# Low parts of the modulation's weight chunks on VectorE, and each modulation row spread one row later, in a two-layer diffusion block

## The reference

```python
def hybrid_layer(x, ctx, c, c_ctx, lw, pos, update_ctx):
    mod_x = jax.nn.silu(c) @ lw['ada_w'] + lw['ada_b']
    mod_c = jax.nn.silu(c_ctx) @ lw['ada_w'] + lw['ada_b']
    shift, scale, gate = jnp.split(mod_x[:, None, :], 3, axis=-1)
    c_shift, c_scale, c_gate = jnp.split(mod_c, 3, axis=-1)
    h = rmsnorm(x, lw['norm_w']) * (1 + scale) + shift
    ...
    x = x + gate * merge_branches(o_m, o_s, o_a, z_m, z_s, z_a, g, lw)
    ...
    # merge_branches, last two lines
    y = jax.nn.sigmoid(g_m) * y_m + jax.nn.sigmoid(g_s) * y_s + jax.nn.sigmoid(g_a) * y_a
    return y @ lw['w_out']
```

## Time and profile before

| | us |
|---|---|
| median of 3 runs | 2136.12 |
| lowest and highest of them | 2133.67, 2136.14 |
| span of the profiled execution | 2133.4 |
| PE busy | 1837.2 (86%) |
| DVE busy | 1210.5 (57%) |
| ACT busy | 889.6 (42%) |
| POOL busy | 602.6 (28%) |

### The profile page before, as it was taken

One profiled execution on the slowest core, in us unless ns is written; L12 is line 12 of the kernel. 1 busy time (PEld: TensorE's weight loads), 2 busy tenths in 40 slices (PEclk: granted clock), 3 DMA queues, 4 the chain that ended last, 5 costly groups with the idle time before them and its releaser, 6 DMA issues.

```text
span 2133.4 us, 27538 instructions
## 1 busy us (share of the span) xinstructions
PE 1837.2 (86%) x10845; PEld 1573.3 (74%) x10845; DVE 1210.5 (57%) x2334; ACT 889.6 (42%) x1679; POOL 602.6 (28%) x328
## 2 busy tenths in 40 slices
PE   5398998879999899998888958989869997899888
PEld 2276787768898788897767946678757886788668
DVE  1524686786666576665232342467867677676334
ACT  1222454544545455544222131344545455555332
POOL 0322221212221222113445132221303323232552
PEclk9699999989999999999999979899989999999999
DMA  6210110101111111113334112011101221122442
GB/s 213 60 46 20 31 27 22 40 11 40 51 50 41 35 35 45 30 41 113 114 103 139 60 62 58 21 34 26 34 20 50 65 65 45 39 61 60 133 138 80
DMA packets 192287, 125.90 MB, mean 59 GB/s; under 512 B 21468, under 2 KB 187934, under 8 KB 192158
## 3 DMA queue, kind: packets, MB, share of 16 engines
q1 hardware_dynamic: 187248, 108.57, 18.0%
q10 hardware_dynamic: 3630, 11.37, 1.4%
q0 software_dynamic: 1280, 4.20, 0.6%
HBM read 119.92 MB, written 4.19 MB: 58 GB/s over the span
## 4 chain that ended last, share of the span: by engine, by line
PE 66%; DVE 19%; ACT 7%; POOL 4%; issue 3%; DMA 1%; ACTq 0%; DVEq 0%; SPq 0%
PE acc L1138 50%; PE wide L1161 5%; PE ptp L1177 4%; DVE nmax L1676 3%; PE pv L1190 3%; DVE e L1693 3%; PE pv L1191 3%; POOL w_lo L1489 2%; DVE pt L1698 2%; ACT e L1402 1%; DVE k_s L1279 1%; ACT w_hi L1321 1%; DVE swapped L1588 1%; DVE rot L1589 1%; DVE q_s L1279 1%
## 5 line engine op out<-in xcount | busy, mean ns | idle before, releaser
L1489 POOL TENSOR_TENSOR w_lo<-w_raw,w_hi 128x1024 fp32r<-128x1024 f32 (+6 forms) x220 | 462.9, 2113 | 1191.3 <-ACT w_hi L1321 1191.1
L1138 PE MATMUL acc<-h_hi,w_hi 128*128 128x512 f32 (+2 forms) x1288 | 472.3, 367 | 43.1 <-POOL w_lo L1489 21.5
L1138 PE MATMUL acc<-h_lo,w_hi 128*128 128x512 f32 (+2 forms) x1288 | 468.2, 364 | 0.0
L1138 PE MATMUL acc<-h_hi,w_lo 128*128 128x512 f32 (+2 forms) x1288 | 466.5, 362 | 0.0
L1138 PEld LDWEIGHTS acc<-h_hi,w_hi 128*128 128x128 f32 (+1 forms) x1288 | 249.2, 194 | 86.0 <-issue 35.9
L1411 ACT ACTIVATE pt<-ptp 128x512 fp32r<-128x512 f32 (+3 forms) x312 | 166.2, 563 | 295.8 <-PE ptp L1177 295.2
L1138 PEld LDWEIGHTS acc<-h_hi,w_lo 128*128 128x128 f32 (+1 forms) x1288 | 248.5, 193 | 38.7 <-issue 1.5
L1138 PEld LDWEIGHTS acc<-h_lo,w_hi 128*128 128x128 f32 (+1 forms) x1288 | 249.1, 193 | 37.6 <-issue 1.3
L1676 DVE TENSOR_REDUCE nmax<-wide 128x1 f32<-128x768 f32 (+3 forms) x240 | 190.5, 794 | 130.7 <-PE wide L1161 129.1
L1321 ACT ACTIVATE w_hi<-w_raw 128x1024 fp32r<-128x1024 f32 (+6 forms) x220 | 199.8, 921 | 78.8 <-DMA w_raw<-in_w_out 67.1
L1402 ACT ACTIVATE e<-wide,nbias,rq 128x768 f32<-128x768 f32 x160 | 145.1, 907 | 172.4 <-DVE nbias L1682 171.8
(11 more groups left out here) (191 smaller groups left out, 3316.1 us busy)
## 6 DMA issues: line engine op xcount, KB each, us to landing
w_raw<-in_w_in SPq DMA_DIRECT2D x102, 512.0 KB, 3.7
w_raw<-in_ada_w SPq DMA_DIRECT2D x48, 512.0 KB, 4.3
w_raw<-in_w_out SPq DMA_DIRECT2D x16, 512.0 KB, 3.8
xres<-in_x ACTq DMA_DIRECT2D x2, 2048.0 KB, 11.2
w_raw<-in_w_o_mla SPq DMA_DIRECT2D x16, 256.0 KB, 2.8
w_raw<-in_w_o_swa SPq DMA_DIRECT2D x16, 256.0 KB, 2.8
w_raw<-in_w_o_ax SPq DMA_DIRECT2D x16, 256.0 KB, 2.8
w_raw<-in_mla_w_uq SPq DMA_DIRECT2D x16, 144.0 KB, 2.4
```

Of the source, the lines that this page charges most:

```text
L1138: ins = nc.tensor.matmul(dst, lhs, rhs, start=first, stop=last)
L1489: nc.gpsimd.tensor_tensor(w_lo[s][:, 0:k], w_raw[s][:, 0:k], f(w_hi[s][:, 0:k]), ALU.subtract).then_inc(w_lo_ready, 1)
```

## The change

`ada()` now returns a row's sums and its spread apart. In the merge, `late()` puts a row's sums down at once, then the spread of the row before it, and keeps its own for the next; the last is put down after the loop. At the head of the program a row is still sums and then spread. Spreads wait for their own row's copy (`row["v"]`) and no longer for everything read so far. The low parts of the rows' chunks (`ada`, 32 in the merges) are made by VectorE at the place of the W event in its order, counted by a semaphore of their own, `ada_lo_ready`; GpSimd makes all others.

```diff
@@ -456,19 +456,26 @@
             whole.update(cc)
         steps = list(group("ada", cost=1900, chunk_ids=cc, act=False, mode="adaF" if plain else "ada", l=l, j=j, slot=slot,
                            needs=lambda: dict(cs_ready=1))["steps"])
-        shape = dict(act=False, l=l, j=j, slot=slot, needs=lambda: dict(acc_free=n["free"], loads=(n["ada"] + 1) // 2))
+        row = {}
+
+        def made_row():
+            row["v"] = n["free"]
+
+        steps += step_of(made_row)
+        shape = dict(act=False, l=l, j=j, slot=slot, needs=lambda: dict(acc_free=row["v"], loads=made // 2 + 1))
+        spread = []
         if j < 2 * D // 256:
-            steps += group("adaT", mode="adaT", **shape)["steps"]
+            spread += group("adaT", mode="adaT", **shape)["steps"]
         else:
             for s in range(len(token_groups(l))):
-                steps += group("adaG", mode="adaG", s=s, **shape)["steps"]
+                spread += group("adaG", mode="adaG", s=s, **shape)["steps"]
         def read():
             ada_made[made] = n["acc"]
             if j == 2 * D // 256 - 1:
                 emit("MOD", l=l, free=n["free"])
                 n["mod"] += 1
-        return steps + [(read, 0)]
+        return steps, spread + [(read, 0)]
     def load_rows(l):
         def run():
@@ -526,7 +533,8 @@
             n["xl"] += 1
             load_table("s")
             for j in COLUMNS:
-                run_all(ada(0, j))
+                row, spread = ada(0, j)
+                run_all(row + spread)
                 if j in (3, 5):
                     norm_rows(0, (j - 3) // 2, 0)
             for tt in range(2, TT):
@@ -679,7 +687,14 @@
         flush()
-        merge = []
+        merge, put_off = [], []
+
+        def late(parts):
+            row, spread = parts
+            got = row + put_off
+            put_off[:] = spread
+            return got
+
         for t in range(KD):
             if t == KD - 2:
                 usable[0] = ROOMY
@@ -690,9 +705,10 @@
             if t == 0:
                 usable[0] = SLOTS
             if t % 2 == 0:
-                merge += ada(l, GATES[t // 2])
+                merge += late(ada(l, GATES[t // 2]))
             if l + 1 < LAYERS:
-                merge += ada(l + 1, t)
+                merge += late(ada(l + 1, t))
+        merge += put_off
         if l + 1 < LAYERS:
             load_table("s")
         run_all(merge)
@@ -846,7 +862,7 @@
         vec_done, vec_ready, consts_ready = semaphore("vec_done"), semaphore("vec_ready"), semaphore("consts_ready")
         cs_th, cs_ready, mod_ready = semaphore("cs_th"), semaphore("cs_ready"), semaphore("mod_ready")
-        w_hi_ready, w_lo_ready = semaphore("w_hi_ready"), semaphore("w_lo_ready")
+        w_hi_ready, w_lo_ready, ada_lo_ready = (semaphore(k) for k in ("w_hi_ready", "w_lo_ready", "ada_lo_ready"))
         acc_done, ev_a, acc_free = semaphore("acc_done"), semaphore("ev_a"), semaphore("acc_free")
         h_done, l_done = semaphore("h_done"), semaphore("l_done")
@@ -936,10 +952,12 @@
         for c in range(len(chunks)):
             loads[c] = (0 if slot_prev[c] is None else loads[slot_prev[c]]) + 16 * len(chunk_dma(c))
-        split_count, splits_to = 0, []
+        split_count, splits_to, lows_to, ada_lows_to = 0, [], [], []
         for c in range(len(chunks)):
             split_count += c not in whole
             splits_to.append(split_count)
+            lows_to.append(sum(chunks[i][0] != "ada" for i in range(c + 1)))
+            ada_lows_to.append(sum(chunks[i][0] == "ada" and i not in whole for i in range(c + 1)))
         @block.sync
         def _(sp):
@@ -1122,9 +1140,12 @@
                             for c in g["chunks"]:
                                 if new(raw_load[slot_of[c]], loads[c]):
                                     pe.wait_ge(raw_load[slot_of[c]], loads[c])
+                        elif mode == "ada":
+                            if new(ada_lo_ready, ada_lows_to[g["chunks"][-1]]):
+                                pe.wait_ge(ada_lo_ready, ada_lows_to[g["chunks"][-1]])
                         elif g["chunks"]:
-                            if new(w_lo_ready, splits_to[g["chunks"][-1]]):
-                                pe.wait_ge(w_lo_ready, splits_to[g["chunks"][-1]])
+                            if new(w_lo_ready, lows_to[g["chunks"][-1]]):
+                                pe.wait_ge(w_lo_ready, lows_to[g["chunks"][-1]])
                         before = g["before"]
                         if before is not None and before["dve"]:
                             if new(acc_free, before["v"]):
@@ -1479,9 +1500,9 @@
             link = splits = tiles = 0
             for e in events:
                 ev = e["ev"]
-                if ev == "W" and e["c"] < len(chunks) and e["c"] not in whole:
+                if ev == "W" and e["c"] < len(chunks) and chunks[e["c"]][0] != "ada":
                     c = e["c"]
-                    splits = splits_to[c]
+                    splits = lows_to[c]
                     k = chunk_size(c)
                     if new(w_hi_ready, splits_to[c]):
                         pool.wait_ge(w_hi_ready, splits_to[c])
@@ -1561,7 +1582,12 @@
             nc.vector.tensor_tensor(cs[:, :, 2:4], silu, f(cs[:, :, 0:2]), ALU.subtract).then_inc(cs_ready, 1)
             for e in events:
                 ev = e["ev"]
-                if ev == "E" and e["g"]["dve"]:
+                if ev == "W" and e["c"] < len(chunks) and chunks[e["c"]][0] == "ada" and e["c"] not in whole:
+                    s = slot_of[e["c"]]
+                    if new(w_hi_ready, splits_to[e["c"]]):
+                        dve.wait_ge(w_hi_ready, splits_to[e["c"]])
+                    nc.vector.tensor_tensor(w_lo[s][:, :], w_raw[s][:, :], f(w_hi[s][:, :]), ALU.subtract).then_inc(ada_lo_ready, 1)
+                elif ev == "E" and e["g"]["dve"]:
                     g = e["g"]
                     kind, src = g["kind"], acc[g["bank"]]
                     tg = g.get("tg")
```

## The result

The changed kernel takes 2139.06 us (median of 20 runs, 2135.39 to 2142.13), the kernel before beside it 2135.78 (20 runs, 2130.41 to 2137.73). The ratio is 1.0017, 95% interval 1.0010 to 1.0023: slower by 3.6 us by the ratio and by 3.3 by the medians, a small loss that is clear of the noise and lies inside the 4.3 us that I called no change. The forecast was 2136.7, 0.6 us over the kernel before.

A forecast was written before the change was run, and what follows sets the result against it. PE, busy for 86% of the span, was taken as the bound. -0.5 - 1.0 + 6.1 - 4.0 = +0.6 gave 2134.3 from the profiled 2133.7, or 2136.7 against the median; range 2131.0 to 2143.5.

The forecast's parts named there:

- Part 4: First layer's tiles 2, 4, 6: waiting bias holds the C row's second chunk in SP's queue; +5.3, with clock +6.1 us.
- The +0.8 for the clock: g_x behind tiles 2, 4, 6: low clock 1.0 each, less the 2.2 tile 4 already paid; +0.8 us.
- rival D: Tiles 2, 4, 6: low clock through sums, spreads and first 4 to 5 us of g_x; +6, 2142.1; 31%.
- Part 3: First layer's tile 0, chunk in time: C sums from 6.4 instead of 8.2, low clock reaching into g_x; -1.0 us.
- Part 2: First layer's tiles 1, 3, 5: only 0.2 gained, the `a_row` wait lying in another's shadow; -0.5 us.
- Part 5: Second layer's merge, four G rows: low-part and `a_row` waits go, g_x at 3.4 instead of 4.4; -4.0 us.
- Part 1: VectorE makes all 32 low parts at 1.21 us each; the one just before `th_x` costed at nothing.
- Rival C: Even tiles: POOL's low part for the next g goes first; tile 0's gain becomes a 0.5 loss; 2138.2; 10%.
- Rival B: Even tiles: chunk in time, as if the queue did not hold it; about -12.5, 2123.6; 10%.

The follow-up runs named there:

- experiment 6: The change with products of no use on PE ahead of its wait before the C sums (12 in tile 0, 24 in tiles 2, 4, 6); 0.9971 of before.
- experiment 1: The change with three places for rows in `a_row` in place of two; ratio 0.9951 to the kernel before.
- experiment 5: The kernel before, with the C row's bias in first-layer tiles 2, 4, 6 made to wait for the G row's sums; ratio 1.0051.
- experiment 8: The change, two places in `a_row`, with the bias behind its row's second chunk in SP's queue; ratio 0.9966 to the kernel before.
- experiment 10: The change, two places, with the row's own spread put down in the same tile at odd tiles; ratio 0.9992 to the kernel before.
- experiment 4: The kernel before with only the rows' low parts moved to VectorE, each spread behind its own sums; ratio 0.9967.
- experiment 2: The kernel before with three places for rows in `a_row`; ratio 0.9996.
- experiment 3: The change's order alone, two places in `a_row`, low parts back on GpSimd; ratio 1.0056 to the kernel before.
- experiment 9: The change's order alone, low parts on GpSimd, with three places in `a_row`; ratio 1.0003 to the kernel before.
- experiment 7: The change with three places in `a_row` and 12 products of no use ahead of the C sums in tiles 0, 2, 4, 6; 0.9921 of before.
- experiment 11: The kernel before with 6 products of no use on PE ahead of the C sums in tiles 0, 2, 4, 6; ratio 1.0013.

## Why the prediction was right, and where its terms were off

**Part 4, the queue: right as a mechanism, too small.** Up to the C sums its steps came as forecast in tile 2: second chunk issued 4.1 after y_x (forecast 4.0), DMA 3.7 (3.7), C sums at 10.1 (10.1). The step that failed is "C sums at the low clock to 13.4, `a_row` and the second spread to 14.5". From the sums' start to g_x it is 5.1, 5.5 and 5.0 in tiles 2, 4 and 6, not 4.4. The sums, up to the first spread, take 3.5 in each, not 3.3. From the first spread to g_x it is 1.56, 2.00 and 1.45, where the forecast had 1.1; the two spreads take 1.3 even at 2.4 GHz (experiment 6, tile 2), so the forecast had them too short, and in tile 4 all four of their products ran at 1.2 GHz, in tiles 2 and 6 the first. In tile 6 the sums also started 0.3 later. The three gaps grew by 7.9 in place of 5.3. Experiments 1, 5 and 8 show the hold as the cause, from three sides.

The +0.8 for the clock behind these gaps is right as a sum and not in its parts, which is luck. The forecast had 1.0 of low clock in each g_x of tiles 3, 5 and 7; it was none in tiles 3 and 7, and 2.9 in tile 5, which had 2.2 in before. So what rival D forecast for all three came in one of them: tile 5's g_x ran at 1.2 GHz for some 6 of its 8.5 us.

**Part 3, tile 0: half right.** C sums at 6.4 and g_x at 11.1 are the forecast's figures. The gap gave 1.4, but tile 1's g_x ran 1.5 longer at the low clock (forecast 0.5): +0.1 in place of -1.0. That 1.5 does not go with the wait alone: experiments 1 and 10 have the same wait of 3.2 and the same gap, and their g_x of tile 1 ran at full clock. The same 1.5 came in tile 6's own g_x, which no term held. So the 5.3 by which the first merge was missed are 2.6 of part 4, 1.1 of tile 0 and 1.5 of tile 6's g_x.

**Part 2, odd tiles:** -0.14, -0.20, -0.14, together -0.5 as forecast.

**Part 5, second layer:** -4.0 as forecast, from -1.0, -1.2, -1.1 and -0.7. The wait for `a_row` is not gone, as the forecast had it in one sentence, but 0.6.

**Part 1, VectorE's low part:** 1.20 to 1.23 in 29 of 32, and 1.7 to 2.2 in the three that started behind one of POOL's. The one ahead of `th_x` is hidden: in all sixteen tiles `th_x` starts 0.04 after the last product of y_x, as in before.

**Rival C:** in tile 0 POOL was 0.17 too late to get in first, so it was not put to the test there. The rule of the Trainium skill, "SBUF — State Buffer", section "Who interferes with whom", is that a VectorE operation with two SBUF inputs and a GpSimd operation that reads SBUF exclude each other, and that the one issued first goes first. It agrees with `y_lo` on 256 columns, 0.41 without a GpSimd low part beside it (experiment 4) and 2.33 with one, and with VectorE's low part, 1.20 ahead of POOL's and 2.23 behind it. **Rival B** needed the chunk in time: that is experiment 1, 0.9951, 10.5 us below before where B had 12.5.

**What came out by luck.** The first merge was 5.3 worse than forecast in the profiled execution. Against it stand 2.2 us less between the merges, where the change alters nothing. It comes from the clock at one place, 700 to 708 us behind tile 7's y_x: the same instructions had a granted clock of 0.53 and 0.62 in before, and 1.00 in the change (two stretches of before, then two of the change):

```profile
1852.00:1856.00 4.00, 2.94 (x14) 2.97 (x15) 2.69 (x6) 0.86 (x4) 0.00 (x0) 0.53 0.10 28
1856.00:1860.00 4.00, 4.00 (x13) 3.23 (x13) 2.55 (x5) 2.63 (x4) 0.22 (x1) 0.62 0.00 0
...
1861.50:1865.50 4.00, 2.28 (x17) 2.22 (x18) 3.73 (x8) 2.12 (x4) 0.00 (x0) 1.00 0.31 94
1865.50:1869.50 4.00, 4.00 (x21) 3.35 (x20) 2.18 (x5) 2.04 (x3) 1.02 (x1) 1.00 0.00 0
```

From tile 7's y_x to the second layer's tile 0 it is 840.3 us in before and 838.2 in the change. It is 840.1 to 840.3 in experiments 2 and 4 too, 838.2 to 838.3 in 1 and 8, and 837.5 to 844.2 over all. No kernel was profiled twice, so whether such a piece goes with the kernel or with the execution stays open; no term of the forecast could have held it. By the medians the whole change is 3.3 and not 4.7, against a forecast of 0.6.

**The range.** The bounds -4.9 and +7.8 give 2131.2 to 2143.9 from the median of 2136.1, not 2131.0 to 2143.5; the measured 2139.06 lies in either.

**The parts against each other**, by the ratios and so to about 2 us: the order with its hold costs 12 us when GpSimd makes the low parts (experiment 3), and 11 when VectorE does (the change against experiment 4). Without the hold the order is worth nothing with GpSimd (experiment 9) and 3 us with VectorE (1 against 4, whose intervals overlap, so that it is not shown). The low parts are worth 7 us with the old order.

## What to carry to other kernels

When code is moved later, look up what waits for it in every queue, a tiny transfer's too, and price all that stands behind that waiter: the 1 KB bias held back 512 KB chunks and cost more than both ideas in the change gave. Put such a waiter behind what is urgent, or give its buffer one place more. Joining several short waits of PE into one long one is no saving if the last of them ends at the same time, and it can cost clock: in experiments 3 and 9 the C sums of tile 0 started when they did before, behind one wait of 4.9 in place of three, and g_x came 1.2 later.

## What was not expected of the hardware

Low clock does not only follow a long idle stretch. At the end of an odd tile PE's last wait is 1.2 to 2.7 us, at a granted clock of 0.95 to 1.00 over the 4 us up to g_x. The g_x behind it ran at full clock in 30 of 42 cases (tiles 2, 4, 6 of fourteen profiles). In the other twelve, among them tile 6 of the change, tile 2 of experiment 7 and tiles 2, 4 and 6 of experiment 11, it ran some 3 us at 1.2 GHz, which costs 1.3 to 1.6. Where these pieces fall changes with edits elsewhere, and filling PE's idle time in experiment 11 took one away in tile 5 and brought three in tiles 2, 4 and 6. What decides their place stays open; they are worth several us in this kernel, as much as the change.

A load of 512 KB took 3.7 from issue to use as the first of a bunch of four (the change, tile 2). In experiment 5 it took 3.6 in tiles 4 and 6 and 5.1 in tile 2, where another row's load was issued before it was in; what made the difference was not tried.
